# Two decoder blocks on one core: the softmax factor of an attention unit computed and applied in the unit's own round

## The chip, the cores and the metric

The kernel runs on one core of one Trainium2 chip. Five engines work beside each other, each on its own in-order queue: TensorE (PE in the profile, its weight loads PEld), VectorE (DVE), ScalarE (ACT), GpSimd (POOL) and SyncE (SP, which here only issues transfers). The metric is the time of one execution in device microseconds (us), as the median of several runs; lower is better.

## The reference

A sequence of 512 tokens of width 1024 goes through one block of a first kind (feed-forward, a mixer that is half sparse attention and half a state-space model, feed-forward, a gated embedding) and two layers of a second kind. Everything is float32. The change lies in the mixer of the first block:

```
z = rmsnorm(h, norm_mix) @ w_in              # q, keys and values of three kinds, gates, u
p_slc = masked_softmax(q k_slc^T)            # kind 1: with 8 blocks of 64 keys and top 16, all causal keys
p_win = masked_softmax(q k_win^T)            # kind 2: a window of 512, again all causal keys
o = g0 * (p_cmp v_cmp) + g1 * (p_slc v_slc) + g2 * (p_win v_win)
state = scan(a_bar * state + bu); y = Re(C state) + d*u       # state-space mixer, 32 groups of 64 states
o_s5 = gelu(y) * sigmoid(gelu(y) @ w_glu + b_glu)
h = h + concat([o, o_s5]) @ w_out
```

## The kernel before

All five engines are programmed by hand. Each has its own function that walks the same list of steps (`mix_order()`, a generator) and does its share of each step; the place of a step in that list is therefore its place in every engine's queue. Waits are on counters: `A.at(...)` waits for ScalarE, `V.at(...)` for VectorE, `P_.at(...)` for TensorE, `G.at(...)` for GpSimd.

Attention is cut into 32 **units**: head pair i (0 to 3), kind (1, 2), query tile qt (0 to 3). Unit n has tile qt = n mod 4 and 128*(qt+1) keys, so its rows are 128, 256, 384 and 512 wide in turn. Each unit has two halves (two heads). Its steps:

- `scores`: TensorE multiplies queries and keys into two PSUM banks and adds the mask (`MASK` matmuls); VectorE takes the negative row maximum of each half (L1895); ScalarE takes the exponential and its row sum into one of four buffers `PB` (L1263).
- `scale`: VectorE takes the reciprocal of both sums (L1901) and multiplies it with the gate (L1904, 128x2: the unit's factor); ScalarE multiplies both halves in `PB` with it (L1271). TensorE does nothing in this step.
- `flip`: TensorE transposes the two halves into two PSUM banks (L776); ScalarE copies them out (L1279), for head pair 3 the second half VectorE (L1910).
- `values`: every fourth unit, TensorE multiplies with the values.

**Round** n of the loop holds `flip` of unit n-2, `scores` of unit n, and other work between. `some(k)` takes the next k steps of the state-space mixer: `scan` (four scans of 128x128 on VectorE, L1805, with two small operations L1810 and L1812), `drive` (two matmuls, four VectorE multiplications of 128x512 from PSUM, L1785 to L1789, two GpSimd additions L2202 and L2204), `back` (one VectorE operation at L1572, then GpSimd L2215, L2217, L2219), `read` (matmuls and one L1572 from PSUM) and `rest`, which holds no instruction at all. A block b of the mixer takes 10 steps, five rounds: scan, scan | scan, scan (with `read` of the block before and both `drive` of the next) | ... | `rest`, `back`(b,0) | `back`(b,1), `scan`(b+1,0). The rounds whose first step is `rest` are 2, 7, 12, 17 and 21; those with both `drive` steps are 1, 6, 11 and 16. After round 22 no such step is left; round 23 holds the GELU (L1299), rounds 25 to 28 the `glu` matmuls with the first loads of `w_out`.

PSUM: seven banks pass through one ring; a matmul group takes the bank that was given back longest ago and waits until its reader is done.

Of the kernel before, what the change touches and what calls it, by code (L numbers as in the profile page):

```python
# [190 lines left out]
def s5_order():  # L191
    for b in range(-1, 9):
        if 0 <= b < 8:
            for c in range(4):
                yield "scan", b, c
        if b >= 1:
            yield "read", b - 1
        if b + 1 < 8:
            yield "drive", b + 1, 0
            yield "drive", b + 1, 1  # L200
        if 0 <= b < 8:
            yield ("rest",)
            yield "back", b, 0
            yield "back", b, 1
# [5 lines left out]
def mix_order():  # L210

    s5 = s5_order()

    def some(n):
        return itertools.islice(s5, n)

    for m in range(4):
        yield "u", m
    yield ("rt",)
    yield from some(2)  # L220
    for i in range(8):
        yield "qk", i
        if i != 1:
            yield "rope", i
        if i == 1:
            yield "turn", 0
            yield "pairs", 0
        if i == 3:
            yield "positions", 0
            yield "pairs", 1  # L230
        if i in (3, 4):
            yield "turn", i - 1
        if i > 5:
            yield "turn", i - 2
        if i >= 4:
            yield "squeeze", 0, i - 4
        yield from some(3)
    yield "positions", 1
    for z in range(2):
        for tt in range(4):  # L240
            yield "v", z, tt
            if z == 0 and tt < 2:
                yield "turn", 6 + tt
            yield from some(1)
        if z == 0:
            yield "compressed", 0
    yield ("gates",)
    work = [(i, kind, qt) for i in range(4) for kind in (1, 2) for qt in range(4)]
    closing = []
    for n in range(34):  # L250
        if closing:
            yield ("values", *closing.pop(0))
        if n > 1:
            if n > 32:
                yield ("scale", *work[n - 2])
                yield ("out_s5",)
            yield ("flip", *work[n - 2])
            i, kind, qt = work[n - 2]
            if qt == 3:
                closing += [(i, kind, part) for part in range(3)]  # L260
        if n < 32:
            if n:
                yield ("scale", *work[n - 1])
            yield ("scores", *work[n])
        if n < 4:
            yield "squeeze", 1, n
        if n == 4:
            yield "compressed", 1
        if 1 < n < 9:
            yield "weigh", n - 2  # L270
        yield from some(2)
        if n == 23:
            assert next(s5, None) is None
            yield ("gelu",)
        if 24 < n < 29:
            yield "glu", n - 25
        if n in (29, 30):
            yield "s5_out", 2 * n - 58
            yield "s5_out", 2 * n - 57
        if n in (30, 31):  # L280
            yield "low", 2 * n - 56
            yield "low", 2 * n - 55
        if n == 30:
            for i in range(3):
                yield "o_part", i
        if n == 31:
            for i in range(3):
                yield "low", i
    for m in range(2):
        yield "out_first", m  # L290
    for x in closing:
        yield ("values", *x)
    yield "out_first", 2


def program(nc, D, out):
    ctx = ExitStack()
    with ctx:
# [258 lines left out]
        def pe_program(e):  # L557
# [78 lines left out]

            hc_banks, v_banks, out_bank, score_banks = {}, {}, {}, {}
            for step, *at_ in mix_order():
                if step == "u":
                    give(w_in(at_[0]), V, "u", at_[0])  # L640
# [446 lines left out]
        def act_program(e):  # L1087
# [114 lines left out]
            act.dma_start(AR[:, 19072:19456], D["small_w"]).then_inc(*loaded("small_w").up())  # L1202

            for step, *at_ in mix_order():
                if step == "u":
                    hi_next()
# [354 lines left out]
        def dve_program(e):  # L1561
# [203 lines left out]
            stage_end("a")  # L1765

            for step, *at_ in mix_order():
                if step == "u":
                    m, = at_
# [696 lines left out]
```

## Time and profile before

| | |
|---|---|
| median of 3 runs | 2084.02 us (2080.2 to 2085.63) |
| profiled execution, its own time | 2084.16 us |
| span of the profiled execution | 2082.4 us |
| PE / DVE / ACT / POOL busy over the span | 1983.1 / 1244.6 / 846.7 / 362.7 us |
| mean granted TensorE clock | 0.967 of full |

The span is the time from the first to the last instruction, and the execution takes 1.8 us more. Busy shares are over the whole span; the change touches some 200 us of it, from the first `scores` at about 520 us to the first output matmuls at about 720 us, so only views with a window say what bounds it.

### The profile page before, as it was taken

The page shows a single profiled execution, that of the slowest core. Times are in us where ns is not written, and L with a number is a line of the kernel's source. Part 1 is how long each engine was busy: PE and PEld are TensorE (multiplying, and loading weights), DVE is VectorE, ACT ScalarE, POOL GpSimd, SP SyncE. Part 2 cuts the span into 40 slices and gives each one's busy share as a digit, 9 for nine tenths or more (in the row PEclk, how much of TensorE's full clock was granted, in tenths as well). Part 3 has the DMA queues.
Part 4 walks back from the last instruction along what each step waited for, and adds up shares of the span by engine and source line. Part 5 has one row for each costly group of instructions (what it writes and reads, how often), then busy time and mean ns, then how long its engine had stood idle before and what let it go on. Part 6 is the DMA issues. An engine that isn't in the chain of part 4 may idle for free.

```text
span 2082.4 us, 21926 instructions
## 1 busy us (share of the span) xinstructions
PE 1983.1 (95%) x8662; PEld 1525.9 (73%) x8662; DVE 1244.6 (60%) x1646; ACT 846.7 (41%) x1269; POOL 362.7 (17%) x319
## 2 busy tenths in 40 slices
PE   7999999989977899999999899999999899999997
PEld 5888888766533478888888777776788778766886
DVE  5764344598696446665664776916663559445742
ACT  5331333302456543322333447544552357445531
POOL 2000000156244010000101302601301024102002
PEclk9999999998788999999999999999999999999998
DMA  5232232221000134654652322321132222220221
GB/s 178 89 126 80 97 110 93 85 76 62 23 0 1 66 102 162 217 177 162 200 174 61 101 82 78 101 91 41 51 101 91 91 89 81 81 81 31 91 91 61
DMA packets 53318, 196.70 MB, mean 94 GB/s; under 512 B 5985, under 2 KB 6497, under 8 KB 52705
## 3 DMA queue, kind: packets, MB, share of 16 engines
q1 hardware_dynamic: 43200, 160.55, 23.4%
q0 software_dynamic: 7504, 28.58, 4.3%
q10 hardware_dynamic: 2512, 6.18, 0.9%
q8 instruction: 69, 1.13, 0.2%
q14 instruction: 33, 0.26, 0.0%
HBM read 192.14 MB, written 2.10 MB: 93 GB/s over the span
## 4 chain that ended last, share of the span: by engine, by line
PE 77%; DVE 15%; ACT 5%; issue 2%; DMA 1%; POOL 0%; SPq 0%; POOLq 0%; DVEq 0%; ACTq 0%
PE PS L562 76%; DVE AR L1572 3%; DVE WLO L1569 3%; DVE AR L1805 2%; ACT WHI L1098 1%; DVE AR L2054 1%; DVE AR L1895 1%; PE PS L776 1%; DVE AR L2021 0%; DMA RAW<-in_w13a 0%; DVE HNL L1572 0%; DVE AR L1851 0%; DMA RAW<-in_w_out 0%; DVE H L1957 0%; DVE AR L1785 0%
## 5 line engine op out<-in xcount | busy, mean ns | idle before, releaser
L1569 DVE TENSOR_TENSOR WLO<-RAW,WHI 128x1024 fp32r<-128x1024 f32 (+1 forms) x272 | 377.4, 1390 | 513.1 <-ACT WHI L1098 512.8
L562 PE MATMUL PS<-HNH,WHI 128*128 128x512 f32 x1632 | 657.2, 403 | 15.8 <-ACT HNH L1129 13.7
L562 PE MATMUL PS<-HNH,WLO 128*128 128x512 f32 x1632 | 641.2, 393 | 3.8 <-DVE WLO L1569 3.8
L1098 ACT ACTIVATE WHI<-RAW 128x1024 fp32r<-128x1024 f32 (+1 forms) x272 | 297.8, 1095 | 683.7 <-PE PS L562 611.9
L562 PE MATMUL PS<-HNL,WHI 128*128 128x512 f32 x1632 | 437.0, 391 | 0.3
L562 PEld LDWEIGHTS PS<-HNH,WHI 128*128 128x128 f32 x1632 | 309.3, 190 | 95.1 <-issue 19.9
L562 PEld LDWEIGHTS PS<-HNH,WLO 128*128 128x128 f32 x1632 | 309.4, 190 | 77.6 <-issue 7.4
L562 PEld LDWEIGHTS PS<-HNL,WHI 128*128 128x128 f32 x1632 | 307.4, 188 | 66.4 <-DVE HNL L1572 2.6
L562 PE MATMUL PS<-AR 128*128 128x512 f32 (+12 forms) x668 | 193.1, 509 | 7.0 <-DVE SQ L1789 3.6
L2180 POOL TENSOR_TENSOR ACC<-ACC,SQ 128x512 f32<-128x512 f32 x46 | 62.8, 1365 | 785.2 <-ACT SQ L1113 784.2
L562 PEld LDWEIGHTS PS<-AR 128*128 128x128 f32 (+5 forms) x668 | 92.2, 197 | 80.3 <-issue 51.9
L562 PE MATMUL PS<-HIDH,WHI 128*128 128x512 f32 x352 | 136.9, 389 | 0.0
L562 PE MATMUL PS<-HIDH,WLO 128*128 128x512 f32 x352 | 136.9, 389 | 0.0
L1572 DVE SCALAR_TENSOR_TENSOR AR<-AR,VEC 128x512 f32<-128x512 f32 x112 | 91.5, 817 | 3.7
L562 PE MATMUL PS<-HIDL,WHI 128*128 128x512 f32 x352 | 90.2, 389 | 0.0
L562 PEld LDWEIGHTS PS<-HIDH,WHI 128*128 128x128 f32 x352 | 66.1, 188 | 13.7
L562 PEld LDWEIGHTS PS<-HIDL,WHI 128*128 128x128 f32 x352 | 66.1, 188 | 13.7
L562 PEld LDWEIGHTS PS<-HIDH,WLO 128*128 128x128 f32 x352 | 66.1, 188 | 13.7
L1805 DVE TENSOR_TENSOR_SCAN AR<-AR 128x128 f32<-128x128 f32 x128 | 71.6, 621 | 0.8
L2188 POOL DMA_DIRECT2D AR<-in_w_ada x48 | 25.3, 528 | 267.4 <-DVE MOD L1713 244.3
L562 PE MATMUL PS<-YRH,WHI 128*128 128x512 f32 x192 | 69.8, 391 | 0.0
L1181 ACT ACTIVATE TMP<-TMP 128x512 f32<-128x512 f32 x44 | 27.8, 632 | 94.1 <-DVE TMP L1740 94.1
(311 smaller groups left out, 2446.3 us busy)
## 6 DMA issues: line engine op xcount, KB each, us to landing
RAW<-in_w_in SPq DMA_DIRECT2D x80, 512.0 KB, 3.5
AR<-in_w_ada POOLq DMA_DIRECT2D x48, 512.0 KB, 3.9
RAW<-in_w13a SPq DMA_DIRECT2D x44, 512.0 KB, 3.3
RAW<-in_w13b SPq DMA_DIRECT2D x44, 512.0 KB, 3.6
RAW<-in_w_out SPq DMA_DIRECT2D x40, 512.0 KB, 3.6
RAW<-in_w2a SPq DMA_DIRECT2D x16, 704.0 KB, 4.1
RAW<-in_w2b SPq DMA_DIRECT2D x16, 704.0 KB, 4.3
RAW<-in_w_inA SPq DMA_DIRECT2D x12, 512.0 KB, 3.4
```

Of the source, the lines that this page charges most:

```text
L562: return pe.matmul(o, l, r, start=start, stop=stop, skip_group_check=True)
L776: t = pe.transpose(ps[:, P * kb:P * kb + P], PB[:, u, P * kb:P * kb + P], IDENT)
L1098: act.activation(hi_of(name, i), raw_of(name, i), ACT.Copy).then_inc(*HI.up(name, i))
L1181: act.activation(TMP[:, q, :], TMP[:, q, :], ACT.Silu).then_inc(*A.up("silu", z, half, mi))
L1569: dve.tensor_tensor(lo_of(name, i), raw_of(name, i), f32(hi_of(name, i)), S_).then_inc(*LO.up(name, i))
L1572: return dve.scalar_tensor_tensor(out=o, in0=a, scalar=s, in1=b, op0=op0, op1=op1)
L1805: dve.tensor_tensor_scan(out=v, data0=rho, data1=v, initial=0.0 if c == 0 else E3[:, z, j:j + 1], op0=M_, op1=A_).then_inc(*V.up("scan", b ...
L1895: dve.tensor_reduce(ST[:, qt % 2, 0, hf:hf + 1], bank("scores", i, kind, qt, hf)[:, 0:P * (qt + 1)], AXX, ALU.max, negate=True).then_inc(* ...
L2054: dve.tensor_tensor_scan(out=CX[:, m, :], data0=RX[:, m, :], data1=IX[:, m, :], initial=0.0, op0=M_, op1=A_).then_inc(*V.up("rg_h", l, m))
L2180: pool.tensor_tensor(ACC, ACC, SQ[:, k % 2, :], A_).then_inc(*G.up("sq", st, k))
L2188: pool.dma_start(STMP[:, 1024 * (c % 2):1024 * (c % 2) + 1024], D["w_ada"][c]).then_inc(ada_sem[c % 2], 16)
```

## The change

In a round of before, the step `scale` is that of the unit before (n-1) and stands ahead of `scores` of unit n. In the changed kernel `scores` of unit n comes first, then one mixer step, then `scale` of the same unit n, then the round's other work, then the second mixer step. The special case for the last units goes, since unit 31 is scaled in its own round.

```diff
         if n > 1:
             if n > 32:
-                yield ("scale", *work[n - 2])
                 yield ("out_s5",)
             yield ("flip", *work[n - 2])
@@
         if n < 32:
-            if n:
-                yield ("scale", *work[n - 1])
             yield ("scores", *work[n])
+            yield from some(1)
+            yield ("scale", *work[n])
         if n < 4:
             yield "squeeze", 1, n
         if n == 4:
             yield "compressed", 1
         if 1 < n < 9:
             yield "weigh", n - 2
-        yield from some(2)
+        yield from some(1)
```

No instruction is added or removed, and the queues of GpSimd and SyncE are the same as before. The file of the changed kernel is one line shorter above these functions, so its line numbers are one lower.

TensorE's queue differs in one place, round 1. Before (two drives of two matmuls each are the `128x512 x4`; `128x62 x8` is `squeeze`):

```order
L562 MATMUL PS<-MASK 128x128 x2
L562 MATMUL PS<-AR,RAW 128x62 x8
L562 MATMUL PS<-AR 128x512 x4
L776 MATMUL PS<-CONST,HX 128x128 x2
L562 MATMUL PS<-AR 128x384 x2
```

and in the changed kernel:

```order
L561 MATMUL PS<-MASK 128x128 x2
L561 MATMUL PS<-AR 128x512 x2
L561 MATMUL PS<-AR,RAW 128x62 x8
L561 MATMUL PS<-AR 128x512 x2
L775 MATMUL PS<-CONST,HX 128x128 x2
L561 MATMUL PS<-AR 128x384 x2
```

The first of the two drives now stands ahead of the squeeze.

VectorE's queue in rounds 11 to 13. Before, from the last two operations of round 11's second drive to the first scan step of the next mixer block (listed as `SCALAR_TENSOR_TENSOR ... x4` at L1805):

```order
L1788 TENSOR_TENSOR AR<-PS,AR 128x512
L1789 TENSOR_TENSOR ACC<-PS,AR 128x512
L1901 RECIPROCAL AR<-AR 128x2
L1904 TENSOR_TENSOR AR<-AR 128x2
L1895 TENSOR_REDUCE AR<-PS 128x1 x2
L1572 SCALAR_TENSOR_TENSOR SQ<-AR 128x512
L1901 RECIPROCAL AR<-AR 128x2
L1904 TENSOR_TENSOR AR<-AR 128x2
L1895 TENSOR_REDUCE AR<-PS 128x1 x2
L1572 SCALAR_TENSOR_TENSOR ACC<-AR 128x512
L1805 SCALAR_TENSOR_TENSOR AR<-AR 128x128 x4
```

and in the changed kernel, from the end of the first drive of round 11 on:

```order
L1788 TENSOR_TENSOR SQ<-PS,AR 128x512
L1900 RECIPROCAL AR<-AR 128x2
L1903 TENSOR_TENSOR AR<-AR 128x2
L1784 TENSOR_TENSOR AR<-PS,AR 128x512
L1786 TENSOR_TENSOR RS<-PS,AR 128x512
L1787 TENSOR_TENSOR AR<-PS,AR 128x512
L1788 TENSOR_TENSOR ACC<-PS,AR 128x512
L1894 TENSOR_REDUCE AR<-PS 128x1 x2
L1900 RECIPROCAL AR<-AR 128x2
L1903 TENSOR_TENSOR AR<-AR 128x2
L1571 SCALAR_TENSOR_TENSOR SQ<-AR 128x512
L1894 TENSOR_REDUCE AR<-PS 128x1 x2
```

The pair of reciprocal and factor moved from behind a round's two mixer steps to between them: in round 11 it now parts the two drives, and in round 12, whose first mixer step is empty, it stands directly behind the two maxima.

ScalarE's queue around the GELU of round 23. Before:

```order
L1263 ACTIVATE HX,AR<-PS,AR 128x512 x2
L1299 ACT_TABLE_LOAD
L1299 ACTIVATE AR<-AR 128x512 x4
L1279 ACTIVATE HX<-PS 128x3x128 x2
L1271 ACTIVATE HX<-HX,AR 128x512 x2
L1263 ACT_TABLE_LOAD
```

and in the changed kernel:

```order
L1262 ACTIVATE HX,AR<-PS,AR 128x512 x2
L1270 ACTIVATE HX<-HX,AR 128x512 x2
L1298 ACT_TABLE_LOAD
L1298 ACTIVATE AR<-AR 128x512 x4
L1278 ACTIVATE HX<-PS 128x3x128 x2
L1262 ACT_TABLE_LOAD
```

The scaling of unit 23 moved from behind the GELU and the copies of unit 22 to ahead of both.

## Rows read from the trace of the kernel before

**Rows 1.** Windows: busy us (instructions) of PE, PEld, DVE, ACT, POOL; clock; DMA.

```profile
560.00:600.00 40.00, 31.08 (x160) 13.91 (x160) 35.19 (x79) 18.87 (x54) 12.58 (x10) 0.83 0.00 1
600.00:640.00 40.00, 31.41 (x164) 13.60 (x160) 35.78 (x74) 22.51 (x65) 24.58 (x19) 0.91 0.00 1
```

**Rows 2.** Waits from 520 to 730 us: total us, times, longest.

```profile
ACT HX L1271 <- DVE AR L1904: 50.9, 25, 4.7
...
PE PS L776 <- ACT HX L1271: 21.8, 7, 5.8
...
DVE AR L1895 <- PE PS L562: 9.4, 9, 1.9
```

**Rows 3.** Timeline of DVE and POOL, rounds 11 to 13: start, us, engine, line.

```profile
602.72 0.68 DVE L1785 TENSOR_TENSOR AR<-PS,AR 128x512 f32<-128x512 f32 x1
602.93 1.27 POOL L2204 TENSOR_TENSOR AR<-AR,SQ 128x512 f32<-128x512 f32 x1
605.11 0.16 DVE L1901 RECIPROCAL AR<-AR 128x2 f32<-128x2 f32 x1
605.30 0.16 DVE L1904 TENSOR_TENSOR AR<-AR 128x2 f32<-128x2 f32 x1
605.38 1.27 POOL L2204 TENSOR_TENSOR AR<-AR,ACC 128x512 f32<-128x512 f32 x1
605.56 0.69 DVE L1895 TENSOR_REDUCE AR<-PS 128x1 f32<-128x128 f32 x2
...
607.55 0.17 DVE L1901 RECIPROCAL AR<-AR 128x2 f32<-128x2 f32 x1 [0.36 <-ACT HX L1263]
...
609.31 0.95 DVE L1895 TENSOR_REDUCE AR<-PS 128x1 f32<-128x256 f32 x2 [0.97 <-PE PS L562]
...
611.36 4.49 DVE L1805 TENSOR_TENSOR_SCAN AR<-AR 128x128 f32<-128x128 f32 x4
613.87 1.38 POOL L2219 TENSOR_TENSOR AR<-AR 128x512 f32<-128x512 f32 x1
```

**Rows 4.** Timeline of DVE, the next scan step, with GpSimd idle.

```profile
617.87 1.61 DVE L1805 TENSOR_TENSOR_SCAN AR<-AR 128x128 f32<-128x128 f32 x4
```

**Rows 5.** Timelines of DVE and POOL, round 2: a factor behind a `back` step.

```profile
541.31 1.25 DVE L1904 TENSOR_TENSOR AR<-AR 128x2 f32<-128x2 f32 x1
541.28 1.26 POOL L2219 TENSOR_TENSOR AR<-AR 128x512 f32<-128x512 f32 x1 [5.17 <-DVE AR L1901]
```

**Rows 6.** PE by itself, rounds 1 and 2: window (PE busy, granted clock) and timeline.

```profile
528.00:529.00 1.00, 1.00 (x3) 0.77 0.00 0
...
532.16 1.65 PE L562 MATMUL PS<-AR 64*128 64x384 f32 x4 [1.92 <-DVE ACC L1789]
```

**Rows 7.** Timelines of DVE and PE, rounds 21 and 22.

```profile
655.25 1.25 DVE L1904 TENSOR_TENSOR AR<-AR 128x2 f32<-128x2 f32 x1
658.47 0.62 PE L562 MATMUL PS<-ACC,AR 128*32 128x512 f32 x1 [1.48 <-DVE ACC L1572]
```

**Rows 8.** Timelines of DVE, ACT and PE, rounds 23 to 25.

```profile
667.07 0.17 DVE L1901 RECIPROCAL AR<-AR 128x2 f32<-128x2 f32 x1 [0.84 <-ACT HX L1263]
668.35 2.19 ACT L1299 ACTIVATE AR<-AR 128x512 f32<-128x512 f32 x4
670.44 0.85 ACT L1279 ACTIVATE HX<-PS 128x384 f32<-128x384 f32 x2
671.18 1.32 ACT L1271 ACTIVATE HX<-HX,AR 128x512 f32<-128x512 f32 x2
672.04 1.94 PE L776 MATMUL PS<-CONST,HX 128*128 128x128 f32 x8 [5.78 <-ACT HX L1271]
675.26 3.68 PE L562 MATMUL PS<-AR,RAW 128*128 128x512 f32 x8
```

**Rows 9.** Timeline of PE, rounds 32 and 33: last transposes, first output matmuls.

```profile
715.96 1.32 PE L776 MATMUL PS<-CONST,HX 128*128 128x128 f32 x6 [2.88 <-ACT HX L1271]
...
720.13 1.09 PE L562 MATMUL PS<-OL,WHI 128*128 128x512 f32 x4
```

## The prediction

> **What bounds the kernel now.** I read three views, narrowed to the stretch that the change touches. First the busy windows [rows 1]: from 560 to 640 us VectorE is busy 35.19 and 35.78 of 40 us, TensorE about 31. The rest of VectorE's time is mostly the hand-over between dependent small operations. So here VectorE is the bound, not TensorE, although TensorE leads the whole page. Second the table of waits [rows 2]: ScalarE waits 50.9 us for the factor L1904 before it can scale, and TensorE in turn waits 21.8 us for scaled rows before it can transpose. That is the time that the change seems to aim at. But the third row says that VectorE itself waits for TensorE's scores only 9.4 us in all. Where the bound engine hardly waits, a wait of the others is slack. Third the timelines, from which four stretches follow:
>
> - 532 to 567 us, rounds 2 to 6: TensorE has no gap after its wait of 1.92 us for a bank, and its clock has just fallen to the lower of its two levels, 1.2 of 2.4 GHz (0.77 in the microsecond of the fall) [rows 6]. TensorE-bound.
> - 567 to 658 us, rounds 6 to 22: VectorE-bound, with places where VectorE is held by GpSimd: a scan step that takes 1.61 us with GpSimd idle [rows 4] takes 4.49 us while GpSimd works off the `back` operations, the last of which is the row at 613.87 [rows 3].
> - 658 to 675 us: a chain through TensorE's last `read` [rows 7] and the GELU, with TensorE idle 5.78 us [rows 8].
> - 675 to 720 us: TensorE with `glu`, the loads of `w_out`, then the tail, with one wait of 2.88 us for scaling [rows 9].
>
> **The change part by part.** Nothing is added; each unit's factor pair (L1901 and L1904) costs VectorE the 0.45 us from 605.11 to the next maximum at 605.56 [rows 3], before as after. What moves is what it delays and what it waits for.
>
> *TensorE's 21.8 us of waiting* for scaling go away almost wholly: the factor of unit n now comes in round n and its transpose in round n+2. Inside the VectorE-bound stretch this gives nothing but the few waits that VectorE has for scores; one such is 0.97 us in round 13 [rows 3]. It is worth 0 there, for the next reason.
>
> *Rounds 12 and 13, and 17 and 18.* The end of the first scan step of a block is set by GpSimd: six `back` operations in a row behind the two drives. VectorE loses 4.49 - 1.61 = 2.9 us in the scan to them [rows 3, 4]. Whatever VectorE does or waits for before that scan lies in this shadow. Removed: the waits of 0.36 and 0.97 us, both in the shadow, 0. Added: a wait of the reciprocal for its own exponential, since in round 12 `rest` puts it straight behind the maxima; by the nearest rows 0.36 us (with a `back` operation between) to 0.84 us (nothing between, unit of 512, [rows 8]); also in the shadow, 0. Once per block a third factor pair moves into the shadow, -0.45; but the pair between the drives makes GpSimd's second pair of additions start later, +0.4. Net about -0.1 per block, -0.3 for three. Without the shadow the added waits would cost 0.5 to 0.8 us each.
>
> *Round 7 and 8.* The new wait of up to 0.84 us (unit 7 is 512 wide) faces a loss that goes: a factor behind the first `back` takes 1.25 us instead of 0.16, since it starts 0.03 us after a GpSimd operation and lasts as long as that [rows 5]. That loss moves to behind the second `back`, where before the scan behind it had it. I take 0, with 1 us either way.
>
> *Round 1.* The pair stands ahead of the second drive, whose last operation (L1789) frees the bank for which TensorE waits at 532.16 [rows 6], and behind that TensorE is the bound. +0.4 us. TensorE's own swap there (a drive ahead of the squeeze) fills no gap of that wait; 0.
>
> *Rounds 20 to 22.* No drive and no scan follow, so there is no shadow: the last `back` releases TensorE's last `read` at 658.47 [rows 7]. The factor of unit 20 now stands directly behind the last scan, where GpSimd starts its `back` operations, and can be held by them for 1.1 us; unit 21 adds a wait for its exponential of 0.36 to 0.84 us, longer if ScalarE is still copying; gone are one pair of 0.45 us and the 1.1 us that the factor at 655.25 was held [rows 7]. I take +0.7, bounds -1 and +2.
>
> *The GELU.* Scaling of unit 23 moves ahead of it. The exponential ends at 667.07, where the reciprocal that waited 0.84 us for it starts; the factor and the two scalings (1.32 us) put the table load and GELU at about 668.9; from 667.05 to 670.54 they took 3.5 us, so they end at 672.4 [rows 8]. TensorE can then transpose unit 23 at 668.2 instead of 672.04, but the scores of unit 25 need the banks of unit 22's copies, behind the GELU: those end at 673.2 (671.3 before), and 1.4 us of scores later `glu` starts, at 674.6 instead of 675.26: -0.6. Against it TensorE has just idled again, and part of the 3.68 us of `glu` may run at 1.2 GHz where it ran at 2.4 before: up to +1.8. I take +0.3.
>
> *The tail.* The transposes at 715.96 no longer wait 2.88 us. But the output matmuls behind them wait next for the low parts of the mixer's output (the OL matmuls at 720.13, [rows 9]), and VectorE makes these in round 31 behind the factor of unit 31, which now waits for its exponential. The gain is given back within a few us: -0.2.
>
> **One thing the rows leave open.** In rounds 1, 6, 11 and 16 the pair now parts the two drives. The reciprocal would start where the second drive's first operation does, at 602.72, and the factor 0.19 us later, as from 605.11 to 605.30: at 602.91. GpSimd's second addition starts at 602.93 [rows 3]. Before, the factor started 0.08 us ahead of such an addition (605.30 against 605.38) and was not held; 0.03 us behind one it was held for 1.1 us [rows 5]. With 0.02 us ahead it can go either way. I take not held (0), bound +1.1 to +1.4 in each of four rounds, since GpSimd's chain and the bank of round 1 both hang on the second drive. The Trainium skill's page SBUF — State Buffer, section Who interferes with whom, says that between a VectorE instruction with two SBUF inputs and a GpSimd instruction that reads SBUF, issue order decides and the second "fully blocks". By that rule a factor that is first costs nothing here and one that is second waits the whole addition; the two rows at 541.28 and 541.31 agree with it, at 1.25 us for 256 numbers.
>
> **Sum.** +0.4 - 0.3 + 0 + 0.7 + 0.3 - 0.2 = +0.9 us on the profiled execution's own 2084.16 us (span 2082.4 and 1.8 around it), which lies 0.14 above the median of 2084.02. Forecast 2085.0 us: no difference that a measurement tells. I take 0.3%, 6.3 us, as what it can tell.
>
> **Rivals.**
> - *The waits of TensorE were the bound after all.* For it: 21.8 us of waits [rows 2], and after 658 us TensorE is the engine that idles, 5.78 and 2.88 us [rows 8, 9]. If those 8.7 us and the waits of rounds 12 to 18 (about 2) come out, 2084.2 - 10.7 = 2073.5. Against it: VectorE's 35 of 40 us, the banks behind the GELU, the low parts behind the tail. 0.09.
> - *The clock of the first stretch.* Rounds 2 to 6 run at 1.2 GHz after an idle stretch of TensorE in round 1. In the new order the first drive fills part of it. If the clock stayed at 2.4 GHz, up to half of the 35 us from 532 to 567 would go; I estimate 11 us, since VectorE's own work binds before the half is reached: 2074. Against: the wait of 1.92 us stays. 0.04.
> - *The factor is held between the drives, and the new waits for exponentials are not in the shadow.* Held 1.4 us in four rounds is 5.6; with the +0.9 it is 2090.7, just past the bound, and it decides from 1.35 us a round on. For it: the margin is 0.02 us and the same in every block, so all four go one way. Held, and rounds 7, 12 and 17 also pay 0.6 each, 2092.5. Chance of this above 2090.3: 0.15; held but below it (2087 to 2090): 0.12.
> - *No change beyond 3 us either way*: 0.60.
>
> **How the numbers follow.** Cases one to three and the last add to 1. Faster by over 0.3%: 0.09 + 0.04, less a little for a partial gain that ends within 6.3 us: 0.12. Slower by over 0.3%: 0.15, and 0.02 for terms of rounds 20 to 25 at their upper bounds together: 0.17. Same: 0.71. The range leaves out the two fast cases (0.13) and the part of the slow one above 2091 (under 0.07): 2080 to 2091.
>
> **What would show it.** In the profile of the changed kernel ACT's wait for L1903 should fall from 50.9 to under 20 us and TensorE's for scaling from 21.8 to under 5, while the span stays; VectorE busy from 560 to 640 us should stay above 34 of 40; a new row should appear of the reciprocal L1900 waiting for L1262, about 5 to 9 us; the factor between drives should last 0.16 us (if 1.2, the third rival holds); `glu` should start within 1 us of 675.3 plus the shift so far, and the output OL matmuls near 720. The prediction is wrong if VectorE's busy share in the middle falls, if the clock stays at 2.4 GHz from 532 us on, or if the last `read` starts more than 3 us away from 658.5.

## The result and the profile after

| | before | changed |
|---|---|---|
| median | 2084.02 us (2080.2 to 2086.39, 5 runs) | 2092.42 us (2089.01 to 2096.9, 5 runs) |
| ratio | | 1.0046, 95% interval 1.003 to 1.0062 |
| profiled execution, its own time | 2084.16 us | 2089.01 us (the fastest of the five) |
| span, mean granted clock | 2082.4 us, 0.967 | 2087.2 us, 0.963 |

The changed kernel is slower, by 8.4 us in the medians. The forecast was 2085.0 us.

The same windows of the changed kernel as in [rows 1] (columns as there):

```profile
560.00:600.00 40.00, 29.91 (x142) 12.78 (x140) 31.42 (x69) 17.88 (x47) 12.97 (x10) 0.79 0.00 1
600.00:640.00 40.00, 35.08 (x150) 15.65 (x148) 33.46 (x71) 21.42 (x59) 22.60 (x18) 0.74 0.00 0
```

VectorE, the bound of this stretch, fell from 35.19 and 35.78 us busy to 31.42 and 33.46, and the clock of the second window from 0.91 to 0.74. The table of waits of the changed kernel from 520 to 730 us, against [rows 2]:

```profile
ACT HX L1270 <- DVE AR L1903: 37.3, 32, 2.5
DVE AR L1894 <- PE PS L561: 21.2, 13, 2.9
DVE AR L1900 <- ACT HX L1262: 17.7, 15, 7.0
...
PE PS L561 <- ACT HX L1278: 5.5, 2, 3.2
...
PE PS L787 <- DVE AR L1888: 4.7, 1, 4.7
...
PE PS L561 <- ACT TMP L1278: 4.0, 2, 3.0
...
PE PS L775 <- ACT HX L1270: 3.6, 3, 2.3
```

TensorE's waits for scaled rows (last row) did fall, from 21.8 to 3.6 us. But three rows above it are new: TensorE now waits 9.5 us for ScalarE's copies of transposes (L1278) and 4.7 us for the last operation of `weigh` (L1888). Two larger rows that aren't shown had others like them before: its waits for drives (L1788) are 7.9 us in all and were 7.7, and 5.1 us for VectorE's copy (L1909) at 712 us stand where 3.7 stood. All its waits together hardly change (39.7 us before, 37.7 after). And VectorE's waits for scores rose from 9.4 to 21.2 us. More than half of that rise (2.7 to 9.4) lies ahead of 567 us, where TensorE is the bound and VectorE's waits at another line (L1865) fell from 10.2 to 4.2. What counts is the stretch that VectorE bounds. VectorE's waits there, from unit 6 to unit 22, before (567.50 to 656.60 us):

```profile
DVE AR L1895 <- PE PS L562: 3.9, 3, 1.9
DVE AR L1901 <- ACT HX L1263: 0.4, 1, 0.4
```

and changed (566.07 to 661.62 us):

```profile
DVE AR L1894 <- PE PS L561: 7.1, 5, 2.3
DVE AR L1900 <- ACT HX L1262: 2.9, 4, 0.9
DVE SQ L1786 <- PE PS L561: 0.6, 1, 0.6
```

They rose by 6.3 us, and the stretch grew by 6.5.

**Where it is lost.** A mark that every profile has is the start of VectorE's maxima (L1894) of a unit, in its timeline. Each cell is the time between two such marks in us, so 10.20 under "20 to 22" is the start for unit 22 less that for unit 20. e1 to e17 are the experiments below. The cells come from one profiled execution each; where two kernels have the same code they can still differ, in the first and the last column above all.

| from unit to unit | 0 to 6 | 6 to 10 | 10 to 11 | 11 to 16 | 16 to 20 | 20 to 22 | 22 to 31 |
|---|---|---|---|---|---|---|---|
| before | 44.46 | 27.55 | 3.87 | 27.79 | 22.85 | 7.04 | 58.52 |
| changed | 44.19 | 27.83 | 5.66 | 27.58 | 24.28 | 10.20 | 61.70 |
| changed again (e16) | 44.64 | 27.83 | 5.67 | 27.59 | 24.25 | 10.20 | 60.23 |
| its idle places filled (e9) | 47.91 | 27.85 | 5.60 | 27.44 | 22.99 | 8.67 | 61.82 |
| `weigh` first (e1) | 46.93 | 29.11 | 5.60 | 27.59 | 25.01 | 8.67 | 60.82 |
| factor alone moved (e4) | 47.96 | 27.84 | 5.66 | 27.60 | 23.88 | 7.10 | 62.43 |
| ScalarE's order alone (e15) | 44.58 | 29.49 | 6.22 | 27.78 | 25.06 | 10.23 | 60.30 |
| factor moved, `weigh` ahead (e17) | 44.63 | 28.00 | 3.87 | 27.43 | 22.94 | 7.11 | 61.57 |

From unit 0 to 31 the changed kernel takes 9.4 us longer (201.44 against 192.08). In its profiled execution unit 0 stands 1.2 us earlier, with the same code ahead of it, and what follows the maxima of unit 31 is 3.4 us shorter, so the span shows only 4.8 of it.

**Round 10.** `weigh` (rounds 2 to 8) makes the attention weights of the compressed keys; TensorE transposes them (L787) and multiplies with the values in round 10. VectorE's timeline of the changed kernel in round 8:

```profile
582.06 1.03 DVE L1903 TENSOR_TENSOR AR<-AR 128x2 f32<-128x2 f32 x1
583.12 0.19 DVE L1882 TENSOR_TENSOR AR<-AR 128x32 f32<-128x32 f32 x1
583.35 1.14 DVE L1886 TENSOR_TENSOR AR<-AR,CONST 128x32 f32<-128x32 f32 x1
584.52 2.19 DVE L1888 TENSOR_TENSOR AR<-AR 128x992 f32<-128x992 f32 x1
```

and TensorE's behind it:

```profile
586.86 1.88 PE L787 MATMUL PS<-CONST,AR 128*31 128x128 f32 x8 [4.72 <-DVE AR L1888]
588.67 3.25 PE L561 MATMUL PS<-HX,AR 128*64 128x512 f32 x8
```

The last `weigh` step now stands behind a mixer step and the factor of unit 8. TensorE idles 4.72 us for it, and the values behind take 3.25 us at the half clock where they took 1.73 before:

```profile
587.45 1.73 PE L562 MATMUL PS<-HX,AR 128*64 128x512 f32 x8
```

**Round 22.** ScalarE's timeline of the changed kernel, then TensorE's:

```profile
655.15 0.69 ACT L1270 ACTIVATE HX<-HX,AR 128x128 f32<-128x128 f32 x2 [2.55 <-DVE AR L1903]
655.75 0.57 ACT L1278 ACTIVATE HX<-PS 128x512 f32<-128x512 f32 x1
656.23 0.58 ACT L1278 ACTIVATE TMP<-PS 128x512 f32<-128x512 f32 x1
```

```profile
656.96 1.08 PE L561 MATMUL PS<-HX,AR 128*64 128x512 f32 x1 [3.04 <-ACT TMP L1278]
```

The copies of unit 19's transposes had their input from 653.1 us on, but stand in ScalarE's queue behind the scaling of unit 20, which waits for its factor; TensorE's values wait for the copies. Before, the copies stood ahead of that scaling, and TensorE's values started at 652.86. The factor itself came late for two reasons: a scan of 1.61 us stands ahead of it now, and then it started 0.01 us behind an operation of GpSimd and lasted as long as that (timelines of VectorE and GpSimd):

```profile
652.15 1.61 DVE L1804 TENSOR_TENSOR_SCAN AR<-AR 128x128 f32<-128x128 f32 x4
653.84 1.26 POOL L2214 TENSOR_TENSOR SQ<-AR 128x512 f32<-128x512 f32 x1 [9.78 <-DVE AR L1900]
653.85 1.27 DVE L1903 TENSOR_TENSOR AR<-AR 128x2 f32<-128x2 f32 x1
```

**Unit 16 to 17.** Between units 11 and 20 the loss stands mainly in one step, where TensorE's only new wait is of 0.50 us. The windows from the maxima of unit 16 to those of unit 17, before and changed:

```profile
626.71:632.55 5.84, 3.88 (x23) 1.97 (x21) 5.60 (x12) 3.11 (x9) 3.88 (x4) 1.00 0.00 0
```

```profile
627.14:635.14 8.00, 8.00 (x21) 4.01 (x22) 5.79 (x13) 3.83 (x11) 5.03 (x5) 0.50 0.00 0
```

TensorE was busy 3.88 of 5.84 us at the full clock and is busy all of 8.00 us at the half, so here the clock makes it the bound.

**Around the GELU** TensorE's timeline, against [rows 8]:

```profile
673.35 1.64 PE L775 MATMUL PS<-CONST,HX 128*128 128x128 f32 x8 [2.27 <-ACT HX L1270]
678.22 1.22 PE L561 MATMUL PS<-AR 64*128 64x256 f32 x4 [3.23 <-ACT HX L1278]
...
679.90 5.72 PE L561 MATMUL PS<-AR,RAW 128*128 128x512 f32 x8
```

One wait of 5.78 us became two of 2.27 and 3.23, and the first `glu` takes 5.72 us for 3.68.

### The profile page after: what moved, and what is told of

It is laid out like the page before. It is cut to its first block, busy times and chain, and to the rows that moved or that the text cites. A ratio compares the mean times of both kernels' runs of the same rounds, so it can differ in the third digit from the quotient of the medians.

```text
span 2087.2 us, 21928 instructions
## 1 busy us (share of the span) xinstructions
PE 1990.2 (95%) x8662; PEld 1524.0 (73%) x8662; DVE 1238.9 (59%) x1646; ACT 849.3 (41%) x1269; POOL 362.4 (17%) x319
## 4 chain that ended last, share of the span: by engine, by line
PE 78%; DVE 13%; ACT 6%; issue 2%; POOL 1%; DMA 1%; ACTq 0%; POOLq 0%; DVEq 0%
PE PS L561 77%; DVE AR L1571 3%; DVE WLO L1568 2%; DVE AR L1804 2%; ACT WHI L1097 1%; DVE AR L2053 1%; PE PS L775 1%; DVE AR L1894 0%; DVE AR L2020 0%; ACT HX L1262 0%; DMA H<-in_xT 0%; POOL ACC L2179 0%; DVE H L1956 0%; DVE ACC L1571 0%; DVE AR L1903 0%
## 5 line engine op out<-in xcount | busy, mean ns | idle before, releaser
L561 PE MATMUL PS<-AR 128*128 128x512 f32 (+12 forms) x668 | 199.4, 515 | 9.7 <-ACT HX L1278 3.2
L1804 DVE TENSOR_TENSOR_SCAN AR<-AR 128x128 f32<-128x128 f32 x128 | 67.4, 587 | 0.8
```

The costliest lines, as they stand in the source:

```text
L561: return pe.matmul(o, l, r, start=start, stop=stop, skip_group_check=True)
L1804: dve.tensor_tensor_scan(out=v, data0=rho, data1=v, initial=0.0 if c == 0 else E3[:, z, j:j + 1], op0=M_, op1=A_).then_inc(*V.up("scan", b ...
```

## The experiments

Ratios are to the kernel before on the same chip, with the 95% interval. They go by all executions of both kernels, so they aren't exactly the quotient of two medians. "Own" means that a unit's factor and scaling stand in its own round, as in the change.

**e1: `weigh` first.** The changed kernel, with the round's other work back behind `scores`:

```diff
             yield ("scores", *work[n])
-            yield from some(1)
-            yield ("scale", *work[n])
...
+        yield from some(1)
+        if n < 32:
+            yield ("scale", *work[n])
         yield from some(1)
```

> The changed kernel with squeeze and weigh back directly behind scores; only the factor and scaling stand between the mixer steps. Theory A (part of the loss is that weigh moved behind the scaling: its last operation releases TensorE's first transposes of CE in round 10, which came 1.9 us late and then ran at the lower clock): 1.8 us of the 8.4 come back, 2090 to 2091, and VectorE no longer waits 1.86 us for the scores of unit 11. Theory B (the place of weigh is of no account, all comes from the factor's own place): no change, 2092.

Measured 2089.2 us, 1.0024 (1.0012 to 1.0036). Its step from unit 10 to 11 stays at 5.60. There the late `weigh` is gone, but the values wait 2.83 us for ScalarE's copies behind the scaling of unit 8. So `weigh` behind the factor isn't the only cause. Theory A had 2090 to 2091 us and the step gone; the time is lower and the step isn't gone.

**e2, e3: a part of the units own.** The kernel before with a condition:

```diff
-            if n:
+            if n and not own(n - 1):
                 yield ("scale", *work[n - 1])
             yield ("scores", *work[n])
+            if own(n):
+                yield from some(1)
+                yield ("scale", *work[n])
...
-        yield from some(2)
+        yield from some(1 if n < 32 and own(n) else 2)
```

e2 with `n > 22`:

> Only units 23 to 31 are scaled in their own round; the rest is the kernel before. Theory A (each stretch has its own loss; here the GELU moves behind the scaling of unit 23, and the first glu matmuls run at 1.2 GHz for 5.7 us instead of 3.7, plus about 1 us in the tail): +2 to +3.5, 2086 to 2087.5. Rival (the late rounds only carry on what came before): 2084, within 1.

Measured 2084.6 us, 1.0 (0.9991 to 1.001), though its profile has 61.46 us from unit 22 to 31 where before has 58.52. e3 with `9 < n < 23`:

> Only units 10 to 22 are scaled in their own round. Theory A (copies out of PSUM now wait on ScalarE behind the scaling of the next unit, TensorE waits for them and then runs at the lower clock): about +4, 2087 to 2089.5, with TensorE's wait of some 3 us ahead of the values in round 21 and VectorE's wait for the scores of unit 22. Rival (the loss of the middle was set off by the late transposes of round 10): +1 or less.

Measured 2086.06 us, 1.0014 (1.0005 to 1.0023), between the two theories. Theory A's mechanism is in its profile, where TensorE's values of round 22 wait 2.11 us for the copies: from unit 16 to 20 it takes 24.58 us and from 20 to 22 8.67, together 3.4 more than before.

**e4: VectorE's factor alone.** Behind `scores` stands `some(1)` and a step `factor` with VectorE's part of `scale`; ScalarE's scaling keeps its old place.

```diff
             yield ("scores", *work[n])
+            yield from some(1)
+            yield ("factor", *work[n])
...
-        yield from some(2)
+        yield from some(1)
```

> The two halves of the step parted: VectorE makes the factor in the unit's own round, between the mixer steps, and ScalarE scales where it did before, behind the copies of the unit before that. Squeeze and weigh stand behind the factor as in the changed kernel. Theory A (ScalarE's new order is the cause of the middle and late losses): GELU and copies are back where they were, only round 10 stays late: 2085 to 2087. Rival B (VectorE's new waits for its own exponentials are the cause): 2090 or more.

Measured 2091.86 us, 1.0033 (1.002 to 1.0046): nearly the whole loss, with ScalarE's order untouched. Of its 10.4 us from unit 0 to 31 only 3.0 lie between units 6 and 22; 3.5 lie ahead and 3.9 behind.

**e5, e6, e8: filling TensorE's idle places.** After these runs I took the half clock for the carrier: in the changed kernel TensorE stood at 1.2 GHz in stretches where before it had 2.4. Matmuls that serve nothing were put ahead of its waits:

```diff
+                elif step == "warm":
+                    for _ in range(at_[0]):
+                        mm(STAT[:, :], ONES, COS, True, True)
```

> The changed kernel with 36 matmuls that serve nothing (each 512 columns of f32 out of two constants into the statistics bank, which nobody reads in the mixer; 0.43 us each by the spacing of such matmuls at the full clock), put on TensorE's queue only where the trace of the changed kernel shows it idle: 6 ahead of the transposes of unit 6, 2 ahead of those of unit 7, 8 ahead of the transposes of the compressed weights in round 10 (its 4.72 us), 3 ahead of those of unit 11, 1 and 5 ahead of the values of rounds 14 and 22, 2 ahead of the scores of round 16, 4 and 5 in round 25. Theory A (the half clock after TensorE's new idle places carries the loss): the granted clock is full in the stretches 64 to 76 and 102 to 114 us after unit 0's maxima and over the GLU matmuls (3.7 us again for 5.72), and the time falls by 4 to 8 us, to 2084 to 2088. Theory B (the order of VectorE's and ScalarE's queues carries it, the clock only follows): the matmuls move nothing or cost 1 to 2 us, 2092 to 2094.

Measured 2091.17 us, 1.0031 (1.0019 to 1.0043). The price was wrong: eight take 7.09 us, 0.89 each, by its row in TensorE's timeline, so they ran past the wait:

```profile
584.13 7.09 PE L567 MATMUL PS<-CONST 128*128 128x512 f32 x16
```

> The kernel before with the same kind of matmuls, 36 of them, in its own idle places: 4 ahead of the scores of unit 7, 6 ahead of the transposes of unit 7, 4, 5 and 7 ahead of those of units 11, 13 and 18, 10 in the 5.78 us ahead of those of unit 23. Theory A: the low stretch from 48 to 64 us after unit 0's maxima goes, and with it 2 to 4 us: 2080 to 2082. Theory B: no change or a loss of 1 to 2 us, 2084 to 2086.

Measured 2084.68 us, 1.0003 (0.9994 to 1.0013).

> The changed kernel with one such matmul ahead of the transposes and one ahead of the scores in each of rounds 7 to 31 (50 in all, 21.5 us of TensorE's time at the full clock), with no regard to where it is idle. TensorE is idle for about 20 to 25% of these rounds, 1.2 us of each. Theory A: some stretches of half clock go, but the matmuls stand in the way in the full rounds; 2086 to 2094. Theory B: a loss of 5 to 15 us, 2097 to 2107.

Measured 2106.38 us, 1.0104 (1.0086 to 1.0122): at 0.89 us each the 50 matmuls are 44 us of work, and stand in the way.

**e7: units 0 to 9 own.**

> The kernel before with the factor and scaling of units 0 to 9 alone in their own round (and so behind them squeeze, compressed and weigh, as in the changed kernel). If the loss of the change is a sum over its places: 8.4 less what units 10 to 22 (+2.0) and 23 to 31 (+0.6) gave alone, +5 to +6, 2089 to 2090. If it is an interaction (the rounds beyond only lose when the first have moved the state-space mixer against the attention rounds): +0 to +2, 2084 to 2086. The marks: at the maxima of unit 10 +0 as in the changed kernel; what comes behind unit 10 tells the two apart.

Measured 2089.07 us, 1.0019 (1.0009 to 1.0029). The three parts (e7, e3, e2) add to 1.0033, the whole was 1.0046 and in e16 1.003: about a sum over places, with more than half of it ahead of unit 10, though each part has an interval of 0.001 either way.

**e9, e10: filling again, by the measured price.**

> The changed kernel with idle places of TensorE filled as in the first try, but now by the measured 0.89 us of such a matmul (7.1 us for 8), so that each group ends before the wait that it stands ahead of does: 3 and 1 ahead of the transposes of units 6 and 7, 4 ahead of those of the compressed weights in round 10, 1 ahead of those of unit 11, 1 ahead of the values of round 14, 1 ahead of the scores of round 16, 2 ahead of the values of round 22, 2 and 3 in round 25; 18 in all. The first try had its 8 run 1.3 us past the wait in round 10, and 2 us over in round 8. Theory A (the half clock in these stretches is the loss from unit 6 on): the mixer from unit 6 to unit 31 lasts about as long as in the kernel before (147.6 us), +0 to +3 of it, and the time falls by 3 to 6 us against the changed kernel, 2087 to 2089. Theory B (the order of the queues): the mixer from unit 6 on keeps +6 or more, with the clock full, and the time stays at 2090 to 2093. Neither touches the first rounds (0 to 6).

Measured 2089.5 us, 1.0025 (1.0014 to 1.0036). One window of it:

```profile
560.00:600.00 40.00, 32.34 (x164) 13.55 (x162) 32.12 (x71) 17.33 (x48) 12.97 (x10) 0.99 0.00 1
```

The clock is full, 0.99 for 0.79 in the changed kernel, but VectorE is as little busy as there (32.12 against 31.42). The table says where the clock counted: from unit 16 to 20 the loss is gone (22.99), from 20 to 22 half of it (8.67), from 10 to 11 nothing (5.60). From unit 6 to 31 it takes 6.75 us more than before, where the changed kernel takes 9.6 and its second run (e16) 8.2. So theory A falls as the main cause there.

> The kernel before with its idle places filled by 0.89 us matmuls that end before the waits do: 2 ahead of the scores of unit 7, 3, 2, 3 and 3 ahead of the transposes of units 7, 11, 13 and 18, 1 ahead of the values of round 18, 5 ahead of the transposes of unit 23; 19 in all. Theory A: 1 to 3 us faster than before, 2081 to 2083. Theory B, and also if the half clock of the kernel before lies only where TensorE isn't what the others wait for: the same as before within 1 us.

Measured 2085.53 us, 1.0002 (0.9992 to 1.0012). The half clock of the kernel before costs nothing that these medians can tell.

**e11, e12: the first rounds and the `weigh` rounds.** `n < 4` and `3 < n < 10`:

> The kernel before with the factor and scaling of units 0 to 3 alone in their own round, so in the half-clock stretch, with the squeeze matmuls behind them. If the loss of units 0 to 9 (+5.4) is the drive's matmuls and squeeze matmuls done after the clock has fallen instead of ahead of it: +2 to +4, and the maxima of units 2 and 3 come 1 to 3.5 us later. If it is the weigh steps of rounds 2 to 8 behind the factor: +0 to +1.

Measured 2086.88 us, 1.0016 (1.0007 to 1.0025), so the first rounds cost, as the first theory has it. Unit 2 comes 1.0 us later and unit 6 2.9.

> The kernel before with units 4 to 9 alone in their own round. If the weigh steps behind the factor (rounds 4 to 8) and the late compressed weights of round 10 carry the loss of units 0 to 9: +3 to +5, with a mark of +1.8 between the maxima of units 10 and 11. If the first rounds carry it: +1 to +2, that mark alone.

Measured 2085.91 us, 1.0012 (1.0003 to 1.0021), between the two theories, with the step of 5.70 from unit 10 to 11 as foretold.

**e13, e14: a few places or spread?** `n % 4 or n < 8`, and `n % 4 == 0 and n > 7`:

> The changed kernel with units 8, 12, 16, 20, 24 and 28 scaled at their old place. These are the units whose round comes just ahead of the one in which the values of a finished block of four are multiplied: in the changed kernel the copies of the block's last transposes (L1278) stand behind such a unit's scaling, and in round 8 the last weigh step stands behind its factor. Theory P (a few places): the mark of +1.8 between the maxima of units 10 and 11 goes, the 3.04 us ahead of the values of round 22 and the split wait around GELU too; from unit 6 to unit 31 +2 to +4 are left of +6.8 (clock filled) to +9.6, and the time is 3 to 5 us below the changed kernel's, 2087 to 2089. Theory Q (spread: each own round costs VectorE its wait for the exponential, 0.53 to 0.93 us each): most of it stays, 2090 to 2092.

Measured 2091.18 us, 1.0025 (1.0013 to 1.0037). That lies in the range of theory Q, and the step from unit 10 to 11 isn't gone but 8.40 us.

> The kernel before with units 8, 12, 16, 20, 24 and 28 alone scaled in their own round. Theory P: +3 to +5, 2087 to 2089, with the maxima of unit 11 1.8 us later. Theory Q: +0 to +2, 2084 to 2086.

Measured 2089.32 us, 1.0017 (1.0007 to 1.0027), by its time and its step of 6.19 theory P. From unit 6 to 31 these six units alone bring 7.1 us (154.73 against 147.62), and the other 26 without them 10.0 (157.66), where all together bring 9.6. Neither theory has that: parts that interleave don't add. It may be that one late unit in a group is enough; no run shows this by itself.

**e15: ScalarE's order alone.** Every unit own, but behind the second mixer step. VectorE's order and TensorE's are those of before up to unit 22:

```diff
-            yield from some(1)
-            yield ("scale", *work[n])
...
-        yield from some(1)
+        yield from some(2)
+        if n < 32:
+            yield ("scale", *work[n])
```

> Every unit's factor and scaling in its own round, but behind the round's second mixer step. VectorE's order is then that of the kernel before up to unit 21, and TensorE's too; ScalarE alone differs, with each unit's scaling ahead of the copies of the unit before. If ScalarE's order carries part of the loss: +2 to +4, 2086 to 2088. If the loss is VectorE's factor between the mixer steps (its waits for exponentials, the weigh steps behind it), as the run with the factor alone moved says: same as before, +0 to +1, up to unit 22, and no more than 2085.5 in all.

Measured 2094.76 us, 1.0041 (1.0028 to 1.0053). I had expected 2086 to 2088 at most; it is the whole loss again, without e4's cause. From unit 6 to 22 it takes 98.78 us, where the changed kernel takes 95.55 and before 89.10: with the factor behind both mixer steps ScalarE's scaling, and the copies behind it, come later still. ScalarE's timeline ahead of the values of round 10, and TensorE's:

```profile
586.91 0.69 ACT L1271 ACTIVATE HX<-HX,AR 128x128 f32<-128x128 f32 x2 [4.45 <-DVE AR L1904]
587.51 1.06 ACT L1279 ACTIVATE HX<-PS 128x512 f32<-128x512 f32 x2
```

```profile
588.72 1.97 PE L562 MATMUL PS<-HX,AR 128*64 128x512 f32 x4 [3.94 <-ACT HX L1279]
```

ScalarE idles 4.45 us for the factor of unit 8 with unit 7's copies behind, and TensorE's values wait 3.94 us for these.

**e16: the changed kernel again.**

> The changed kernel once more, as it is, on the chip of the other three: how much of its loss a second profile repeats. From the other runs that share its first rounds: the maxima of unit 6 at +2.5 to +6.3 us (in its first profile -0.3), those of unit 11 1.8 later still, from unit 6 to unit 31 +9 to +10; the median 2091 to 2093. If the first profile was typical, unit 6 stands at -0.3 again.

Measured 2091.79 us, 1.003 (1.0018 to 1.0041). Behind unit 6 its steps repeat to 0.03 us up to unit 22. Unit 6 stands at +0.2, near the -0.3 of the first profile and not at the +2.5 to +6.3 that I expected. From unit 6 to 31 it takes 8.2 us more than before, for the +9 to +10 expected.

**e17, e18: both orders kept.** The factor alone moves, as in e4, but behind `weigh`:

```diff
         if 1 < n < 9:
             yield "weigh", n - 2
-        yield from some(2)
+        yield from some(1)
+        if n < 32:
+            yield ("factor", *work[n])
+        yield from some(1)
```

> The kernel before with one thing moved: VectorE's factor stands in the unit's own round between the mixer steps, as in the run with the factor alone, but the weigh steps keep their place ahead of it; ScalarE's scaling and TensorE's order are those of before. Of the two queue orders found so far, neither is in it: the last weigh step isn't behind the factor of unit 8, and the copies of the transposes aren't behind the next scaling. What is left is VectorE's waits for exponentials (0.84, 0.53, 0.63 and 0.93 us in rounds 7 to 20, some 1.6 us more around GELU). If the two orders carry the loss: from unit 6 to unit 31 +1 to +3 instead of +6.9 and +11.5 with one of them, no step of 1.8 us between units 10 and 11, and 2084.5 to 2087 us. If the factor between the mixer steps costs by itself, through VectorE's waits and the later drives: +5 to +7 again, 2089 to 2092.

Measured 2084.36 us, 1.0012 (1.0001 to 1.0022). Its windows:

```profile
560.00:600.00 40.00, 32.62 (x151) 14.25 (x148) 35.52 (x73) 19.57 (x52) 13.99 (x11) 0.79 0.00 1
600.00:640.00 40.00, 32.46 (x168) 13.97 (x166) 35.90 (x74) 22.72 (x63) 26.59 (x20) 0.87 0.00 1
```

VectorE is busy 35.52 and 35.90 us again. The clock of the first window is 0.79, as in the changed kernel, and does no harm. From unit 6 to 22 it takes 89.35 us, before 89.10; VectorE waits 5.0 us there, before 4.3. From unit 6 to 31 it is +3.3, just past the +1 to +3 of the first expectation, and 3.0 of that lies behind unit 22. The interval of its ratio lies below the changed kernel's first one and overlaps that of e16, so it is the steps, more than the medians, that show what came back.

> The same with the 19 filling matmuls of the second try on the kernel before, at the same places. If the half clock is a consequence of TensorE's idle places and adds to what they cost: 1 to 3 us less than the kernel without them. If TensorE isn't waited for there: the same within 1 us.

Measured 2087.15 us, 1.0019 (1.0007 to 1.003): not better than e17, with overlapping intervals. None of these kernels beats the one before.

## Why the prediction was wrong

The forecast was 2085.0 us, range 2080 to 2091; the median came out at 2092.42. The sum was +0.9. It took 0.1 us of gain for three blocks, though only two were named (rounds 12 and 13, 17 and 18). Its terms against the marks of the changed kernel and of its second run (e16):

| stretch | forecast | measured, first and second |
|---|---|---|
| round 1 (unit 0 to 2) | +0.4 | +0.9, +1.4 |
| units 2 to 6 | 0 | -1.2, -1.2 |
| units 6 to 10 | 0, 1 either way | +0.3, +0.3 |
| unit 10 to 11 | no term | +1.8, +1.8 |
| units 11 to 20 | -0.3 (three blocks) | +1.2, +1.2 |
| units 20 to 22 | +0.7, to +2 at most | +3.2, +3.2 |
| units 22 to 25 | no term | +0.3, +0.3 |
| GELU (unit 25 to 26) | +0.3 | +1.4, +1.4 |
| units 26 to 31 | -0.2 | +1.5, +0.1 |

**The step that failed** is "TensorE's 21.8 us of waiting", which I let go "almost wholly" and then followed no further. I costed what the moved instructions delay on VectorE and GpSimd, and named for each what was queued behind it there. On ScalarE I did so at the GELU alone. In every other round, too, the copies of unit n-2's transposes, which had stood ahead of the scaling of unit n-1, now stand behind it. Nor did I see that `weigh` moves behind a mixer step and a factor. Both release TensorE, so its waits changed their releaser and hardly their sum. What I had put at no term (unit 10 to 11) is +1.8 us, and what I had put at +0.7 (units 20 to 22) is +3.2. "Where the bound engine hardly waits, a wait of the others is slack" was true of the kernel before and used up by the change: between units 6 and 22 VectorE's waits rose from 4.3 to 10.6 us, and the stretch by as much.

That these two orders carry the loss between units 6 and 22 is shown. With VectorE's alone (e4) the step at unit 10 is 5.66 us and the one at 20 to 22 stays at 7.10. With ScalarE's alone (e15) they are 6.22 and 10.23. With neither (e17) they are 3.87 and 7.11, as before, although the factor stands between the mixer steps there too. Taking away one of the two in round 10 shows nothing (e1: 5.60), since the other is about as late. The two don't add up either: over units 6 to 22 the changed kernel loses 6.5 us, e4 3.0 and e15 9.7.

**What TensorE's clock added.** The +1.2 between units 11 and 20 is mostly its work: filled, these rounds take 50.43 us (e9), before 50.64. From unit 16 to 17 the time goes with the granted clock: 5.84 us at 1.00 before, 5.97 at 1.00 in e17, 6.20 at 0.72 in e9, and 8.0 at 0.50 in both profiles of the changed kernel. The orders count there too: e4, with ScalarE's old order, takes 7.05 at the same 0.50. At 20 to 22 it doubled what the order began: 10.20 us at 0.83 in these two, 8.67 at 0.95 to 0.98 in e1, e3 and e9, of which e1 and e3 have no filling, and 7.05 at 1.00 before. Why the clock fell just there isn't shown. By the medians of e9 and e16, whose intervals overlap, the clock can't be told from nothing. The forecast had priced it at GELU alone: `glu` took 2.04 us more where I had put "up to +1.8" and counted little of it. The start of `glu` itself was right: 4.6 us later than before where units 22 to 24 are 5.0 later, so -0.4 for the -0.6 that was forecast.

**The first rounds.** By the medians units 0 to 3 alone cost 0.16% (e11), some 3 us, where I had +0.4 for round 1. The profiles scatter, so that no single one gives this term. From unit 0 to 6, with the old order in these rounds, six took 44.5 to 44.6 us (before, e2, e3, e6, e12, which differs from unit 4 on, and e15, where the scaling alone moves), e14 46.1 and e10 47.5. With the changed order the changed kernel took 44.2 and 44.6, e1 46.9, e11 47.4, e5 and e9 47.9, e7 and e8 50.7 (e13 lacks a record here). With the factor alone moved it was 48.0 (e4), 44.6 (e17) and 40.2 (e18).

This goes with how long TensorE stood at its lower level between the two marks: 20.5 us in e18, 27.3 in the two of the changed kernel, 30.7 in the six at 44.5 and in e17, 34.1 in e1 and e11, 37.5 in e10, e4, e5 and e9, 41.0 in e7 and e8. It isn't exact: e14 took 46.1 with 27.3. At the same 37.5 us the old order took 47.5 and the changed one 47.9, a difference of the size that I had forecast. So what e11 lost by its median is either a longer stay at the lower level or lies elsewhere. What would make that stay longer is argued and not shown: work that had been done ahead of the fall of the clock comes behind it. The cause of this part of the loss stays open.

**Behind unit 22** the causes aren't told apart. e17 loses 3.0 us there with the factor alone, e15 1.8, e2 2.9, and e2's median shows none of it. So it is open whether this part is in the medians at all. One part is VectorE's waits for exponentials; the row `DVE AR L1900 <- ACT HX L1262` rose from 7.6 to 17.7 us, where I had expected 5 to 9. Another is the half clock of `glu`, 2.0 us.

**The rivals.** The third named 2090.7 to 2092.5 us, which is where the time came out, but by luck, since its reason didn't happen. The factor between the drives isn't held, as the changed kernel's timelines of VectorE and GpSimd show

```profile
631.19 0.16 DVE L1903 TENSOR_TENSOR AR<-AR 128x2 f32<-128x2 f32 x1
631.20 1.30 POOL L2203 TENSOR_TENSOR AR<-AR,SQ 128x512 f32<-128x512 f32 x1
```

with the same 0.16 us, 0.01 to 0.02 ahead of GpSimd, in the other three blocks. Its waits for exponentials did come, 2.9 us between units 6 and 22 for 0.4 before, but e17 has 1.8 us of them and loses 0.2 there. With the rule of the Trainium skill (page SBUF — State Buffer, section Who interferes with whom) which I had cited, that issue order decides, the trace agrees: here the factor came first, and at 653.85 it came second and took 1.27 us. The first rival (waits were the bound) and the second (a full clock in the first stretch) fell: the waits were moved and not removed, and TensorE stood at its lower level for 27.3 us of that stretch, before for 30.7.

**Its own signs.** Right: TensorE's waits for scaling under 5 (3.6), factor between drives 0.16, `glu` where the shift puts it. Wrong: ScalarE's wait for the factor under 20 (37.3), VectorE above 34 of 40, the OL matmuls near 720 (727.36), VectorE's new row of 5 to 9 us (17.7), the last `read` within 3 us of 658.5 (663.49). VectorE's share and the last `read` were the signs that I had given for being wrong.

## What to carry to other kernels

When an instruction moves ahead in an in-order queue, write down for each engine that issues part of it what stands behind it now and didn't before, and who waits for that; the wait that the move removes comes back under another releaser (21.8 us for scaling became 3.6, and 14.2 for copies and weights). The test of such a move is the sum of the waits of the engine that bounds the stretch, not the row that one meant to cut: all of TensorE's waits together fell by 2 us here while the kernel got slower, and VectorE's between units 6 and 22 rose by 6.3. If taking one suspect away changes nothing, take both away before acquitting either: in round 10 two releasers were about equally late, and only e17, without both, showed them.

## What the runs showed of the hardware

**A full clock needn't be worth anything.** From 560 to 600 us, eight of e9's 18 idle matmuls of 0.89 us went with a granted clock of 0.99 instead of 0.79, and VectorE, the bound, gained 0.7 us of busy time. In the kernel before such a filling changed nothing that the medians tell (e10, 0.9992 to 1.0012). Where TensorE becomes the bound it is worth something: 8.0 us from unit 16 to 17 at 0.50, 6.20 at 0.72.

**The half-clock stretch ends at another place from run to run.** The windows from 520 to 560 us of e13 (in these rounds the changed kernel) and of e18 (the order of before but for the factor); before had a clock of 0.62 there:

```profile
520.00:560.00 40.00, 37.98 (x160) 27.95 (x161) 22.51 (x61) 17.04 (x44) 12.53 (x10) 0.53 0.07 20
```

```profile
520.00:560.00 40.00, 36.56 (x206) 23.43 (x204) 27.55 (x74) 17.68 (x47) 12.50 (x10) 0.74 0.11 32
```

In e13 TensorE is busy 37.98 of 40 us and stands at the lower level nearly all the time. In e18 the higher level came back early, and unit 6 stood 4.4 us ahead of e17's (40.20 us behind unit 0 for 44.63), whose code is the same up to there. The Trainium skill's page TensorE: Matmul & The Clock Gate, section What's actually happening, says that the moment of the change varies between runs of one kernel; the traces agree, and here that moment is worth 4.4 us, more than most edits of this study.
